# Opening a mixture of experts with a pair of fixed experts in place of four, and closing it with a pair

## What is computed

```python
def block_fn(args):
    tok, wt, e = args
    xb = x2[tok]
    hb = jax.nn.silu(xb @ w_gate[e]) * (xb @ w_up[e])
    return (hb @ w_down[e]) * wt[:, None].astype(xb.dtype)
```

## Time and profile before

| | us |
|---|---|
| median of 3 runs | 1529.62 (1529.06 to 1530.7) |
| the profiled execution | 1531.76 |
| its span in the trace | 1528.4 |
| TensorE busy | 1429.0 (93%) |
| VectorE busy | 326.9 (21%) |
| ScalarE busy | 225.6 (15%) |
| read from HBM | 477 MB |

### The profile page before, as it was taken

How to read it: one execution, slowest core, us unless ns; L and a number is a source line. 1 busy time by engine, 2 the same in 40 slices (tenths; PEclk the granted TensorE clock), 3 DMA queues, 4 the chain that set the end, 5 groups by cost and what they waited for, 6 DMA issues and landing times.

```text
span 1528.4 us, 15897 instructions
## 1 busy us (share of the span) xinstructions
PE 1429.0 (93%) x6656; PEld 687.7 (45%) x6656; DVE 326.9 (21%) x689; ACT 225.6 (15%) x482; POOL 11.4 (1%) x54
## 2 busy tenths in 40 slices
PE   7999999999899999999999999999789889879886
PEld 6889876776544553343324334223124224214222
DVE  2096510173731031111210111111011001100103
ACT  2001120144510111111101001001001001001002
POOL 1000000000000010000000000000000000000000
PEclk9999999999999999999999999999999999999999
DMA  9755563433427268999999998999999999999994
GB/s 301 221 166 165 165 212 120 117 75 85 110 83 220 110 275 331 420 423 417 423 422 423 422 415 346 417 423 421 425 423 422 423 423 422 423 422 423 422 423 188
DMA packets 132697, 480.25 MB, mean 314 GB/s; under 512 B 16428, under 2 KB 82192, under 8 KB 82704
## 3 DMA queue, kind: packets, MB, share of 16 engines
q1 hardware_dynamic: 126112, 476.54, 80.0%
q10 hardware_dynamic: 6512, 2.68, 0.7%
HBM read 477.09 MB, written 2.10 MB: 314 GB/s over the span
## 4 chain that ended last, share of the span: by engine, by line
PE 73%; DMA 18%; SPq 3%; DVE 3%; ACT 1%; issue 1%; ACTq 0%; DVEq 0%
PE PS L1072 19%; PE PS L845 13%; PE PS L1089 11%; DMA ring<-in_expert_w_up_dram 8%; DMA ring<-in_expert_w_down_dram 7%; PE PS L942 7%; PE PS L1063 5%; PE PS L1106 4%; PE PS L834 4%; SPq L557 3%; PE PS L865 3%; DMA spare<-in_expert_w_down_dram 2%; PE PS L884 1%; PE PS L917 1%; PE PS L1078 1%
## 5 line engine op out<-in xcount | busy, mean ns | idle before, releaser
L1072 PE MATMUL PS<-ring,XG 128*32 128x512 f32 (+1 forms) x1792 | 402.9, 597 | 51.3 <-DMA ring<-in_expert_w_up_dram 47.3
L1072 PEld LDWEIGHTS PS<-ring,XG 128*32 128x32 f32 (+1 forms) x1792 | 106.6, 119 | 320.8 <-issue 231.4
L1089 PE MATMUL PS<-ring,hTe 128*32 128x512 f32 (+1 forms) x912 | 203.9, 595 | 7.2 <-DMA ring<-in_expert_w_down_dram 3.8
L845 PE MATMUL PS<-hT,ring 128*128 128x256 f32 x768 | 166.6, 379 | 0.0
L845 PEld LDWEIGHTS PS<-hT,ring 128*128 128x128 f32 x768 | 145.8, 190 | 20.2 <-issue 0.5
L1089 PEld LDWEIGHTS PS<-ring,hTe 128*32 128x32 f32 (+1 forms) x912 | 53.6, 118 | 151.5 <-issue 114.7
L942 PE MATMUL PS<-ring,mix 128*128 128x512 f32 x256 | 113.0, 600 | 1.1 <-ACT mix L1388 1.1
L2081 DVE TENSOR_TENSOR hTe<-PS,sg 128x128 f32<-128x128 f32 (+1 forms) x33 | 11.0, 332 | 434.9 <-ACT sg L1571 434.9
L1969 DVE TENSOR_TENSOR x<-PS,x 128x1024 f32<-128x1024 f32 x44 | 53.9, 1224 | 173.6 <-PE PS L1106 173.5
L1106 PE MATMUL PS<-Y,SW 128*128 128x512 f32 x176 | 88.7, 611 | 0.3 <-ACT Y L1581 0.3
L2088 DVE COPY Y<-PS 32x1024 f32<-32x1024 f32 (+1 forms) x33 | 40.4, 1223 | 215.7 <-PE PS L1089 215.7
(11 more groups left out here) (335 smaller groups left out, 792.0 us busy)
## 6 DMA issues: line engine op xcount, KB each, us to landing
ring<-in_expert_w_down_dram SPq DMA_DIRECT2D x56, 2048.0 KB, 27.3
ring<-in_expert_w_gate_dram SPq DMA_DIRECT2D x108, 1024.0 KB, 24.4
ring<-in_expert_w_up_dram SPq DMA_DIRECT2D x108, 1024.0 KB, 26.5
ring<-in_w_in_dram SPq DMA_DIRECT2D x22, 2048.0 KB, 9.7
spare<-in_expert_w_gate_dram SPq DMA_DIRECT2D x19, 1024.0 KB, 24.3
spare<-in_expert_w_up_dram SPq DMA_DIRECT2D x19, 1024.0 KB, 26.8
spare<-in_expert_w_down_dram SPq DMA_DIRECT2D x8, 2048.0 KB, 27.3
ring<-in_w_out_dram SPq DMA_DIRECT2D x32, 256.0 KB, 7.6
```

The source lines that it names most:

```text
L845: mm = pe.matmul(dst, lhs, rhs, start=(k == 0), stop=(k == DK - 1))
L1072: mm = pe.matmul(PS[64 * u:64 * u + width, 0, :], XG[:, 4 * c + j, column:column + width], w[u][:, j, :], start=(c == 0 and j == 0), stop= ...
L1089: mm = pe.matmul(PS[64 * half:64 * half + width, 2 + b, :], hTe[:, k, 0:width], w[:, j, half * 1024 + b * 512:half * 1024 + (b + 1) * 512] ...
```

## The change

`STATIC` falls from 4 to 2: the fixed experts are 30 and 31, alone in a first group of two steps with 64 columns each, so of 128 columns. Experts 28 and 29 join the sorted ones. Their list grows by two at its small end, and those two make a ninth group, of two steps with 32 columns each. The groups are now 2, 5, 4, 4, 4, 4, 4, 4, 2 steps. The double step moves from steps 11 and 12 to 9 and 10.

The rest makes pairs possible. `OWN` names the half of `Y2` that a group of one half uses; `parts_of` gives a group's parts, with 64 rows for the last. The routing weights of a pair are transposed behind its first step and the next group's `sel` is made there too (`turn_at`, `select_at`). Scatters stay 44: none in the first group, two in each step of the second and third but the fifth of the second, one in each step of the groups of four, two in each step of the last pair, four behind it. The eighth place for a chunk uses the other half of `Y2`.

```diff
-QUADS = [[64] * 4, [64, 64, 64, 32, 32], [64] * 4] + [[32] * 4] * 5
-WIDE = 3
-TWIN = 11
-STATIC = 4
+QUADS = [[64] * 2, [64, 64, 64, 32, 32], [64] * 4] + [[32] * 4] * 5 + [[32] * 2]
+OWN = {0: 1, 3: 0, 4: 1, 5: 0, 6: 1, 7: 0, 8: 1}
+TWIN = 9
+STATIC = 2
...
+def parts_of(q):
+
+    columns = sum(QUADS[q])
+    if columns > P:
+        return [(0, P, 0), (P, P, 1)]
+    return [(0, columns, OWN[q])]
...
     q, i = STEP[s]
-    if q >= WIDE:
-        return [((q - WIDE + 1) % 2, i // 2, i % 2)]
-    if i == 4 or (q == 0 and i < 2):
+    if q == 0 and (len(parts_of(0)) == 1 or i < 2):
+        return []
+    if len(parts_of(q)) == 1:
+        each = 4 // len(QUADS[q])
+        return [(1 - OWN[q], n // 2, n % 2) for n in range(each * i, each * i + each)]
+    if i == 4:
         return []
     return [((i // 2 + 1) % 2, i % 2, cols) for cols in range(2)]
...
+def turn_at(q):
+    return 0 if len(QUADS[q]) == 2 else 1
+
+
+def select_at(q):
+    return 0 if q == 0 and len(QUADS[q]) == 2 else 2
...
-        aside_halves = [Y2[:, 1, :], fin_g[:, :]]
+        aside_halves = [Y2[:, 1 - OWN.get(0, 0), :], fin_g[:, :]]
...
-                    mm = pe.matmul(PS[:, 4 + 2 * cols + b, :], SW[:, buf, t * P:(t + 1) * P],
-                                   Y2[:, buf, (2 * cols + b) * 512:(2 * cols + b + 1) * 512], start=True, stop=True)
+                    mm = pe.matmul(PS[:, 4 + 2 * cols + b, :], SW[0:rows, buf, t * P:(t + 1) * P],
+                                   Y2[0:rows, buf, (2 * cols + b) * 512:(2 * cols + b + 1) * 512],
+                                   start=True, stop=True)
...
-                if STEP[s][1] == 1:
+                if STEP[s][1] == turn_at(STEP[s][0]):
                     turn_weights(s)
...
-                if i == 2 and q + 1 < len(QUADS):
+                if i == select_at(q) and q + 1 < len(QUADS):
                     dve.wait_ge(sw_filled, q + 1)
                     select(q + 1)
```

More of the change, by code:

```diff
@@ L41 @@
 BLOCKS = 9
-QUADS = [[64] * 4, [64, 64, 64, 32, 32], [64] * 4] + [[32] * 4] * 5
-WIDE = 3
-TWIN = 11
-STATIC = 4
+QUADS = [[64] * 2, [64, 64, 64, 32, 32], [64] * 4] + [[32] * 4] * 5 + [[32] * 2]
+OWN = {0: 1, 3: 0, 4: 1, 5: 0, 6: 1, 7: 0, 8: 1}
+TWIN = 9
+STATIC = 2
+RANK_AT = [E - STATIC + v for v in range(STATIC)] + [3, 4, 5, 6, 7, 1, 2, 0, 0] + list(range(8, E - STATIC))
 STEP = [(q, i) for q, quad in enumerate(QUADS) for i in range(len(quad))]
@@ L52 @@
 FIRST = [STEP.index((q, 0)) for q in range(len(QUADS))]
-RANK_AT = [E - STATIC + v for v in range(STATIC)] + [3, 4, 5, 6, 7, 1, 2, 0, 0] + list(range(8, E - STATIC))
 WIDTH_AT = [width for quad in QUADS for width in quad]
 LOAD = [v - (v > TWIN) for v in range(NV)]
+def parts_of(q):
[3 more added lines that the diff above has]
+    return [(0, columns, OWN[q])]
 def column_of(s):
@@ L63, in place_of @@
 def place_of(s):
-    q = STEP[s][0]
-    return (column_of(s) // P, column_of(s) % P) if q < WIDE else ((q - WIDE) % 2, column_of(s))
+    col = column_of(s)
+    return next((buf, col - first) for first, rows, buf in parts_of(STEP[s][0]) if first <= col < first + rows)
 def scatters_at(s):
     q, i = STEP[s]
-    if q >= WIDE:
-        return [((q - WIDE + 1) % 2, i // 2, i % 2)]
-    if i == 4 or (q == 0 and i < 2):
+    if q == 0 and (len(parts_of(0)) == 1 or i < 2):
[4 more added lines that the diff above has]
+    if i == 4:
         return []
     return [((i // 2 + 1) % 2, i % 2, cols) for cols in range(2)]
+def turn_at(q):
+    return 0 if len(QUADS[q]) == 2 else 1
+def select_at(q):
+    return 0 if q == 0 and len(QUADS[q]) == 2 else 2
 ADDS = [(s, *g) for s in range(NV) for g in scatters_at(s)]
-ADDS += [(NV, (len(QUADS) - 1 - WIDE) % 2, t, cols) for t in range(TT) for cols in range(2)]
+ADDS += [(NV, OWN[len(QUADS) - 1], t, cols) for t in range(TT) for cols in range(2)]
 ADDS_AT = [[n for n, g in enumerate(ADDS) if g[0] == s] for s in range(NV + 1)]
@@ L87, in filled_by, with rows_by @@
     return max(s for s in range(ADDS[n][0]) if place_of(s)[0] == ADDS[n][1]) + 1
+def rows_by(n):
+    s = filled_by(n) - 1
+    return next(rows for first, rows, buf in parts_of(STEP[s][0]) if buf == ADDS[n][1])
 def added_by(n, cols):
@@ L1117, in turn_weights @@
                     pe.wait_ge(sc_added, added_by(n, 1))
-                for col in range(0, sum(QUADS[q]), P):
+                for col, rows, buf in parts_of(q):
                     for t in range(TT):
-                        mm = pe.transpose(PS[:, 6, 2 * col + t * P:2 * col + (t + 1) * P], selw[:, t, col:col + P],
-                                          ident[:, :])
+                        mm = pe.transpose(PS[0:rows, 6, buf * T + t * P:buf * T + (t + 1) * P],
+                                          selw[:, t, col:col + rows], ident[:, :])
                 mm.then_inc(sw_filled, 1)
@@ L1203, in _ @@
                 for s in range(FIRST[q], FIRST[q] + len(QUADS[q])):
-                    if s == FIRST[0] + 2:
+                    if ADDS_AT[s] and ADDS_AT[s][0] == 0:
                         pe.wait_ge(blocks_ready, 3)
@@ L1548, in _, with save_gather @@
             act.activation(ro[:, 7, :, 0:EG], ro[:, 6, :, 0:EG], ACT.Exp, bias=ZERO_C).then_inc(route_exp, 1)
-            def save_gather(f, width):
+            def save_gather(f, width, done=g_saved):
                 act.activation(XG[:, 2 * f:2 * f + 2, 0:width],
                                PS[:, 6 + f % 2, :].rearrange("p (k n) -> p k n", k=2)[:, :, 0:width],
-                               ACT.Copy).then_inc(g_saved if width > SLOTS else ov_act, 1)
+                               ACT.Copy).then_inc(done, 1)
             HT = PS[:, 1, :].rearrange("p (k n) -> p k n", k=4)
@@ L1589, in weights @@
                 else:
-                    act.activation(SW[:, (q - WIDE) % 2, :], PS[:, 6, 0:T], ACT.Copy).then_inc(sw_saved, 1)
+                    col, rows, buf = parts_of(q)[0]
+                    act.activation(SW[0:rows, buf, :], PS[0:rows, 6, buf * T:buf * T + T], ACT.Copy)\
+                        .then_inc(sw_saved, 1)
             for s in range(NV):
@@ L1603, in _ @@
                 result(s)
-                if i == 1:
+                if i == turn_at(q):
                     weights(q)
```

11 lines of the change are left out of this document (7 added, 4 removed).

## The result

| | before | after |
|---|---|---|
| time, median us (lowest to highest) | 1529.62 (1526.36 to 1532.97) | 1532.48 (1530.82 to 1536.18) |
| runs | 11 | 11 |
| ratio after/before, 95% interval | | 1.0022 (1.0013 to 1.0030) |
| profiled execution, us | 1531.76 | 1533.97 |
| its span, us | 1528.4 | 1532.1 |

By the ratio the change costs 3.4 us (2.0 to 4.6); the two medians lie 2.9 apart. That is just over what a measurement of this kernel can tell from no change. The forecast was 1534.0, 4.4 us more. For the profiled execution it was 1536.2, with a span of 1532.8; it took 1533.97, with a span of 1532.1. The spans are 0.7 apart, the times 2.2, because 1.9 us stand outside this span and 3.4 stood outside before's.

What follows compares the result with a forecast made beforehand. From about 610 us the stream of expert weights was taken to set the pace. Stream loss 3.0 plus last step 1.4 made 4.4 us on 1529.62, so 1534.0 us; range 1530.0 to 1537.5.

Steps and rivals of the forecast that it cites:

- The first group: Start of the kernel: the first group's fourth gate and up part ends 6.99 us earlier, at 581.33 us.
- `sel`, taken as nothing: Before the first gather: the narrower `sel` saves nothing, as TensorE is at warming products; bounds 0 and 0.3 us.
- The hollow: Wide gather, 620 to 656 us: the weight queue runs dry, near 310 GB/s, with some 10 us of 36 lost.
- The size of the stream's loss: At the wide gather, net of the start's gain: 3.0 us lost, between bounds 2.1 and 3.7.
- the 9.6 us row: Earlier down chunk issued after a stop, 9.6 us to landing; as chunk 23's case it adds 1.6, making 3.7 us.
- the double step: Its dip moves to about 842 to 911 us and costs the stream the same 8 us, near 372 GB/s.
- differs by over 1 us: Sign of being wrong: a double step whose loss differs by over 1 us.
- The last step: Two scatters in place of one add 1.71 us, 0.32 covered, so 1.4 us more; bounds 0 and 1.7.
- The loss is hidden: Rival, 20%: the `fin_g` load falls into the hole, gives back up to 2.4 us; 1531.6, no measurable change.
- The gain stays: Rival, 7%: the stream stays 7 us ahead because the wide gather does not empty the queue; 1524.0 us.
- A slower end: Rival, 12%: the clock falls in the last step, up to 1.7 us, and chunk delays may add as much; 1537.
- The loop: Rival, 1%: an expert over its columns runs the loop behind the last step, over 30 us; 1560 or more.

Runs made afterwards that it cites:

- e3: Changed kernel with the second group's gather taking only the first 128 tokens, so half its products are left out; 1526.02 us, ratio 0.9969 against before.
- e4: Changed kernel with a narrow group of four experts run second and the two wide groups third and fourth; 1523.28 us, ratio 0.9956 against before.
- e2: Changed kernel with the 1 MB load of `fin_g` issued one step earlier, ahead of the wide gather; 1530.74 us, ratio 1.0001 against before.
- e7_changed_again: Changed kernel run again with no edit; 1531.96 us, ratio 1.0017 against before.
- e1_pair_inside: Changed kernel with the last pair of small experts run second to last, so the last step carries one scatter; 1530.84 us, ratio 1.0005 against before.
- e11: Changed kernel with a narrow group run second and the wide groups third and fourth, the same kernel as e4 run again; 1524.71 us, ratio 0.9967.
- e8: Kernel before, with its four fixed experts, with the order alone changed: two narrow groups ahead of the two wide ones; 1530.05 us, ratio 0.9998.
- e10: Changed kernel with a narrow group second, the last pair second to last, and TensorE's part of the skipped loop removed; 1524.49 us, one execution.

## Why the prediction was right, point by point

**The first group.** The fourth part ended 24.88 us after the first gather (555.47 to 580.35), 6.89 less than before's 31.77; the prediction had 6.99. 380 GB/s stand where about 390 were expected.

**`sel`, taken as nothing.** It gave 0.2 us. The start of after's timeline (rank written at 554.67, before at 555.48):

```profile
554.92 0.49 DVE L2017 TENSOR_TENSOR sel<-slot,rank 128x128 f32<-128x128 f32 x2
...
555.52 1.67 PE L1088 MATMUL PS<-sel,xn 128*128 128x128 f32 x13
```

From rank to the first gather product are 0.85 us, before 1.07. The narrower `sel` is written 0.27 us faster (0.49 in place of 0.76), so most of its saving reached TensorE: the argument that the warming products would hold it back was wrong, within its bounds.

**The hollow.** Second step's end 614.07 (predicted 614.90), the wide step's fourth part 643.77 (644.59), chunk 23 issued at 651.46 (652.2), all 0.7 to 0.8 early, as this execution was from the start. 308 GB/s in 620 to 656 us (about 310). The mechanism is shown from three sides: shorten the gather and the stretch fills (e3), move it and it fills (e4), issue something earlier and that fills it (e2).

**The size of the stream's loss** was the step that was off. The prediction took 3.0 us from between 2.1 and 3.7; it was 3.6, and 3.7 when repeated. The chunk itself came at the lower bound: 7.7 us from issue to landing, below even the 8.0 of the earlier trace rows. Counted from the first gather, chunk 23 landed 2.1 us later than before, and the landings behind it tell where the rest of the 3.6 comes from (worked out from the DMA records, each from its own first gather; the load of `fin_g` lies ahead of chunk 60 in all four):

| kernel | chunk 60, later than before's | chunk 60 to 144 | chunk 144 to 191 |
|---|---|---|---|
| before | | 427.2 | 234.1 |
| after | 2.1 | 428.6 | 234.1 |
| e7_changed_again | 2.2 | 428.7 | 234.0 |
| e1_pair_inside | 2.0 | 427.9 | 234.0 |

Chunk 60 lands just ahead of the double step in after, and both kernels are through theirs at chunk 144. So the hollow cost the stream 2.1 us, the lower bound, and the 9.6 us row, for which the prediction added 0.9, did not apply. The other 1.4 us came at the double step, which the prediction put at no change. By the windows it lost 0.7 more, by the landings 1.4 (1.6 in e7, 0.7 in e1); "differs by over 1 us" was named as a sign of being wrong. That 3.0 came near 3.6 is therefore partly luck: a sum for one place stood in for a loss at another. (The bounds of the prediction add up to 1535.0 at the top; its forecast says 1535.5, and nothing hangs on the difference.) Whether that loss belongs to the change is not shown. The three executions have it in different sizes, and e4 and e11, one kernel, differ there by 2.3 us.

**Behind the hollow.** The first wait of TensorE came at 742.02 (predicted near 745), and 911 to 1478 us move 423 GB/s:

```profile
742.02 3.63 PE L1097 MATMUL PS<-ring,XG 128*32 128x512 f32 x16 [1.35 <-DMA ring<-in_expert_w_up_dram]
```

**The last step.** 1.2 us against 1.4. The wait ahead of the last down products is gone, as said. The 0.2 between them are the down products: two rows of 3.63 in the earlier trace rows, 7.26 us, took 7.06 in one piece. The final scatters on 64 rows took 7.13 us in after, on 128 rows 7.10 in before: nothing, as taken.

**The rivals.** "The loss is hidden" was refused for the reason given: ACT issues the load after the hollow. e2 confirms that it is hidden when issued one step earlier, and at the predicted size, 2.4 us. "The gain stays" needed a queue deeper than there was; e4 makes it true by taking the gather away from that place. "A slower end" shows in one profile (e3) at the price given. The loop did not run.

**What stays open.** By the ratios the changed kernel costs 2.6 to 3.4 us, by the cut traces, less `sel`'s 0.2, 4.6 to 4.7. Most of that gap lies in which executions were profiled. Before's span was 1528.4 us, and the median span of its executions beside the experiments is 1528.1. After's was 1532.1 against a median of 1530.7, e7's 1532.6 against 1530.2. So the traces of the changed kernel are long by 1.4 and 2.4 us, and a typical execution need not lose all of the 3.6 us of stream. No run here tells in which stretch it is the shorter one.

## What to carry to other kernels

When a stream of transfers sets the pace, ask of each burst of compute how deep the queue is at that moment: the same wide gather cost nothing behind four full experts (424 GB/s in before's from 671.91 to 701.60 us) and more than the whole gain behind two (308 GB/s in after's hollow, and chunk 23 landed 2.1 us later than before in place of 7 earlier). Here the shorter first stage paid where light groups followed it and the heavy one came behind them, at a full stream (e4: 422 GB/s from 713 to 743 us, 6.7 us under before), and it did not pay with the heavy one right behind it (after: 3.4 us over). The holes that remained were free room for a load that doesn't belong to the stream, issued before the hole (e2: chunk 24 landed 2.4 us earlier) and not after it.

## What the runs showed of the hardware

**The branch over the skipped loop took 0.36 to 3.89 us, by kernel.** The trace's records of TensorE's compare and branch ahead of the loop last 0.37 us in before and 0.36 in e8, and 3.87 us in after (3.32 to 3.89 in all the others that were recorded with the loop). Around it in after two transfers of 16 KB run on the instruction queue. The DMA view of after from 1509 to 1516 us:

```profile
GB/s 0 0 0 0 0 0 0 0 0 0 0 0 0 94 0 0 0 0 0 0 0 0 0 0 0 0 0 0 0 0 0 94 0 0 0 0 0 0 0 0
...
q8 instruction: 2, 0.03, 1.7%
```

One lies at 1511.4, during the branch, and one at 1514.4 us, behind it. In before the first of them had already run at 1503.8, ahead of the branch at 1507.1. The records, in us, with the first of the two transfers:

| kernel | branch | its length | first transfer | branch's end behind the transfer's |
|---|---|---|---|---|
| before | 1507.10 to 1507.47 | 0.37 | 1503.84 to 1504.93 | 2.54 |
| e8_four_fixed_narrow_second | 1507.32 to 1507.68 | 0.36 | 1502.93 to 1504.02 | 3.66 |
| after | 1509.93 to 1513.80 | 3.87 | 1511.41 to 1512.28 | 1.52 |
| e7_changed_again | 1510.45 to 1513.78 | 3.32 | 1511.40 to 1512.27 | 1.50 |
| e2_load_in_gap | 1508.22 to 1511.84 | 3.62 | 1509.16 to 1510.31 | 1.53 |
| e4_narrow_second | 1498.07 to 1501.96 | 3.89 | 1499.58 to 1500.45 | 1.51 |

In all nine executions with a long branch it ends 1.50 to 1.53 us behind the end of the first transfer, however late that transfer starts (0.94 to 1.51 us into the branch). So the long branches' length goes with the start of the transfer. In before and e8 the transfer was over 2.17 and 3.30 us before the branch began.

Most of the branch lies under the down products (1506.45 to 1513.51 us in after), so it shows as 0.35 us of idle time in after and 1.15 in e1, and as none without the loop (e10). The 0.35 cost nothing: from the end of the down products to the first scatter product are 1.39 us in after, 1.38 in e7, where the idle time was a wait for ACT instead, and 1.37 in before. In e1 they are 2.10. Why the first transfer came early in before and e8 and late in the others is not shown, and no run here moves it alone, so that the branch waits for it is a reading of the fixed 1.5 us between them.

**A 2 MB load that meets an empty queue** landed 7.7 us after its issue in after's hollow (7.4 to 8.2 for the same chunk, 23, in e1, e2 and e7) and 8.0 in before at 581.7 us; 4.96 of it is transfer, if it runs at the stream's rate, which leaves 2.7 of the 7.7. Once it was 9.6. The load ahead of chunk 23, issued at 643.81 us with other transfers still running, took 7.5.
